# Writing out seven expert pairs of TensorE's program in place of a loop

## What is computed

```python
def expert_choice_ffn(h, w_router, w_gate, w_up, w_down):
    cap = EC_CAPACITY_FACTOR * T // N_EXPERTS          # 64 latent, 32 context tokens an expert
    aff = softmax(einsum('btd,de->bte', h, w_router))
    gate, idx = lax.top_k(swapaxes(aff, 1, 2), cap)
    xs = h[idx]
    hid = silu(xs @ w_gate) * (xs @ w_up)
    y = (hid @ w_down) * gate[..., None]
    return zeros.at[idx].add(y)
```

## Time and profile before

| What | Value |
|---|---|
| Median of 3 runs | 2056.06 us (2052.41 to 2056.16) |
| The profiled execution: time, span of its instructions | 2060.62 us, 2058.8 us |
| TensorE busy | 1944.4 us (94% of the span) |
| Mean granted TensorE clock | 0.975 |
| Layer 0's looped pairs, first matmul to first matmul of the eighth | 816.33 to 1117.11 us |
| Layer 0's eighth pair up to its `c` matmuls | 1117.11 to 1163.80 us |
| TensorE instruction queue (q8) | 109 packets, 1.79 MB |

### The profile page before, as it was taken

One profiled execution on the slowest core, in us unless ns is written; L12 is line 12 of the kernel. 1 busy time (PEld: TensorE's weight loads), 2 busy tenths in 40 slices (PEclk: granted clock), 3 DMA queues, 4 the chain that ended last, 5 costly groups with the idle time before them and its releaser, 6 DMA issues.

```text
span 2058.8 us, 41161 instructions
## 1 busy us (share of the span) xinstructions
PE 1944.4 (94%) x17601; PEld 1266.4 (62%) x17601; DVE 724.5 (35%) x1507; ACT 507.0 (25%) x1079; POOL 362.7 (18%) x411
## 2 busy tenths in 40 slices
PE   6999999899999998999999899999889999999998
PEld 4565567678888554555555445556688885455554
DVE  3154344344443334111121325334345442523223
ACT  4211533432222222010100131343332222210001
POOL 1512000333341002200010032100135330000000
PEclk7999999999999999999999999999899999999999
DMA  9410000344444215999999612100100002489996
GB/s 326 126 41 21 21 1 1 114 158 153 149 141 145 73 51 175 310 347 312 328 325 316 229 41 62 42 0 21 53 13 13 23 3 104 162 342 408 414 408 263
DMA packets 196888, 320.65 MB, mean 156 GB/s; under 512 B 10761, under 2 KB 163119, under 8 KB 189583
## 3 DMA queue, kind: packets, MB, share of 16 engines
q1 hardware_dynamic: 184928, 287.20, 39.6%
q0 software_dynamic: 6432, 20.00, 3.5%
q10 hardware_dynamic: 5390, 11.44, 1.6%
HBM read 305.45 MB, written 13.16 MB: 155 GB/s over the span
## 4 chain that ended last, share of the span: by engine, by line
PE 82%; DMA 5%; DVE 5%; ACT 4%; issue 2%; SPq 1%; POOL 1%; DVEq 0%; ACTq 0%; POOLq 0%
PE psum L564 16%; PE psum L962 7%; PE psum L1104 5%; PE psum L1056 5%; PE psum L1082 5%; PE psum L684 3%; PE psum L1167 3%; PE psum L893 3%; DMA ring<-in_moe_w_up 3%; PE psum L905 3%; PE psum L1063 2%; PE psum L908 2%; PE psum L729 2%; PE psum L704 2%; PE psum L501 2%
## 5 line engine op out<-in xcount | busy, mean ns | idle before, releaser
L564 PE MATMUL psum<-hT,ring 128*128 128x256 f32 (+2 forms) x976 | 336.8, 502 | 4.2 <-ACT hT L1481 3.8
L564 PEld LDWEIGHTS psum<-hT,ring 128*128 128x128 f32 (+1 forms) x976 | 184.0, 191 | 144.5 <-issue 126.8
L1056 PE MATMUL psum<-ring,arena 128*64 128x256 f32 x1024 | 126.4, 403 | 25.3 <-DMA ring<-in_moe_w_up 15.2
L962 PE MATMUL psum<-hT,ring 128*128 128x512 f32 (+1 forms) x384 | 139.4, 521 | 0.9 <-DVE xT L2261 0.9
L905 PE MATMUL psum<-ring,wbuf 64*64 64x64 f32 x1920 | 123.3, 226 | 3.7 <-DVE wbuf L2226 2.8
L908 PE MATMUL psum<-wbuf,ring 64*64 64x64 f32 x1920 | 121.1, 224 | 0.0
L2533 POOL TENSOR_TENSOR mlaw<-ring,lev 128x512 f32<-128x512 f32 x72 | 91.1, 1270 | 165.0 <-PE psum L893 162.6
L1056 PEld LDWEIGHTS psum<-ring,arena 128*64 128x64 f32 x1024 | 76.3, 145 | 68.8 <-issue 36.7
L2348 DVE TENSOR_TENSOR arena<-arena,psum 128x384 f32<-128x384 f32 (+1 forms) x32 | 15.6, 488 | 291.1 <-PE psum L1063 191.7
L962 PEld LDWEIGHTS psum<-hT,ring 128*128 128x128 f32 x384 | 72.7, 190 | 64.8 <-issue 61.5
L905 PEld LDWEIGHTS psum<-ring,wbuf 64*64 64x64 f32 x1920 | 103.8, 140 | 7.3 <-issue 5.3
(11 more groups left out here) (330 smaller groups left out, 3294.3 us busy)
## 6 DMA issues: line engine op xcount, KB each, us to landing
ring<-in_moe_w_gate SPq DMA_DIRECT2D x64, 1024.0 KB, 10.1
ring<-in_ada_w SPq DMA_DIRECT2D x48, 1024.0 KB, 5.2
ring<-in_moe_w_up SPq DMA_DIRECT2D x48, 1024.0 KB, 8.1
ring<-in_moe_w_down SPq DMA_DIRECT2D x32, 1024.0 KB, 11.2
ring<-in_w_in SPq DMA_DIRECT2D x20, 1024.0 KB, 5.9
big<-in_moe_w_down SPq DMA_DIRECT2D x16, 1024.0 KB, 14.5
ring<-in_w_out SPq DMA_DIRECT2D x8, 1024.0 KB, 5.1
xT<-in_moe_w_up SPq DMA_DIRECT2D x8, 1024.0 KB
```

The costliest lines, as they stand in the source:

```text
L564: m = pe.matmul(b[0:c1 - c0, 0:n], lhsT=w[:, k, c0:c1], rhs=hT[:, k, t0:t0 + n], start=k == 0, stop=k == KD - 1)
L962: m = pe.matmul(b[:, 0:x], lhsT=w[:, k, c:c + P], rhs=mixT[:, k, t0:t0 + x], start=k == OUT_REST[0], stop=k == OUT_GDN[-1])
L1056: m = pe.matmul(b[e * CAP_L:(e + 1) * CAP_L, 0:2 * P], lhsT=xs[:, k, e, 0:CAP_L], rhs=w[e][:, k, :], start=k == 0, stop=k == KD - 1)
```

## The change

The body of TensorE's loop becomes a function, `looped(i)`. In layer 0 (`need_ctx`) it is called seven times by Python with the numbers 0 to 6, so the instructions stand in the program seven times with constant thresholds. Layer 1 keeps the loop. No other engine's program differs except for line numbers.

```diff
-                with pe.Fori(0, PAIRS - 1) as i:
+                def looped(i):
+
                     def claim2(name):
...
                     pair(claim2, done2, weights2, free2, lambda name: ("moe", l, name), i,
                          i * per_pair + 2 * per_pair)
+
+                if need_ctx:
+                    for i in range(PAIRS - 1):
+                        looped(i)
+                else:
+                    with pe.Fori(0, PAIRS - 1) as i:
+                        looped(i)
                 for b in range(BANKS):
                     uses[b] += (PAIRS - 1) * per[b]
```

## The result

The written-out kernel takes 2057.86 us at the median of 20 runs (2049.91 to 2062.91), the kernel before 2052.53 us at the median of 20 beside it (2047.27 to 2058.60). The ratio is 1.0023 with a 95% interval of 1.0012 to 1.0033: 4.7 us slower, 2.5 to 6.8. The profiled execution of after took 2058.16 us, its span is 2056.3. It happens to be quicker than the profiled execution of before, the other way round than the medians. Single runs of one kernel scatter by some 4 us, so the difference is looked for inside the pairs, not between two spans.

The account below looks back on a forecast made before the run. The prediction took each pair to be paced by a closed ring through u0, u1's load and VectorE's additions. Terms 0 + 0.6 − 0.6 + 0.9 = +0.9 us on the 2056.06 us median gave 2057.0 us, range 2050 to 2068.

Parts of the forecast that it names:

- the clock: After some u1 waits the granted clock falls, 1.69 us each; up to three more or fewer, ±5.1 us.
- The branch: Six back edges and one exit removed in layer 0, covered by VectorE's additions: 0, at most 3.0 us.
- The form of g0's wait: Constant thresholds make six inner boundaries start g0 0.14 us after VectorE's addition instead of 0.04: +0.6 us.
- The form of u1's wait: Landing to u1's first matmul takes 0.14 us instead of 0.23, in seven pairs: −0.6 us.
- More code to fetch: 23 more 16 KB code packets add traffic on busy DMA engines: +0.9 us, bounds 0 and 8.4.
- Fetches delay u1's load: Rival: packets make u1's loads land late, up to 1.4 us a pair; with clock falls +13.5 us, 2069.6; chance 0.17.
- Nothing else is idle: In the seven pairs TensorE idles only before u1 (15.2 us) and before g0 at back edges (3.0 us).
- Back edges were dear after all: Rival: idle time at back edges and 0.23 us at u1 all go, −4.6 us, 2051.5; chance 0.13.
- A fetch at the back edge: Rival: each of six returns to the loop's head fetches a packet; writing out saves 7.2 us, 2048.9; chance 0.02.
- TensorE starves at the fetches: Rival: TensorE stops for each of 23 packets, 27.6 us slower, 2083.7; chance 0.04.
- the ring: What paces a layer 0 pair: u0 done, load issued, landed, u1, rest of pair, VectorE's additions, next g0, u0.

Follow-up runs that it names:

- e1_null: The kernel before, unchanged, timed again against itself: ratio 0.9999 (0.9982 to 1.0016), −0.7 us.
- e5_mimic_h0: The looped kernel before plus, in each of layer 0's seven looped pairs, a 16.3 KB copy on ScalarE's queue behind h0: 1.0003, +1.1 us.
- e6_mimic_g0: The looped kernel before plus, in each of layer 0's seven looped pairs, a 16.3 KB copy on ScalarE's queue behind g0: 1.0014, +2.4 us.
- e2_again: The written-out kernel, unchanged, timed again against the kernel before: ratio 1.0014 (0.9996 to 1.0031), +2.6 us.
- e3_both: The written-out kernel with TensorE's loop written out in layer 1 too; against the kernel before 1.0017 (1.0 to 1.0034), +4.2 us.
- e4_single_loops: The written-out kernel with each of layer 0's seven pairs a one-pass loop ending in a branch not taken; against the kernel before 1.0013, +2.4 us.
- e10_place_bad: The written-out kernel plus 9 small matmuls before u1 in seven pairs and 55 ahead of pair 1, setting where fetches fall: 1.0024, +3.8 us.
- e12_warm: The looped kernel before plus one 512-column matmul (four in pair 8) ahead of u1's wait in layer 0: 0.9982 (0.9965 to 0.9999), −3.4 us.
- e8_half_loop: The looped kernel before with only half the columns of each layer 0 down weight loaded: 1.0008 (0.9992 to 1.0025), +1.6 us.
- e7_two_pairs: TensorE's layer 0 as pair 1 written out, then three loop passes of two pairs, thresholds in registers; against the kernel before 1.0073, +15.0 us.

## Why the prediction was right, and which term was off

The forecast was 2057.0 us for a measured 2057.86, and slower by 0.9 us for a measured 4.7 (2.5 to 6.8). That the two times agree within 0.9 us is luck. The forecast started from 2056.06 us, the median of three runs, and the same kernel had 2052.53 in the 20 runs beside after: the start was 3.5 us too high, and the effect 3.8 us too small (4.4 by the medians). The measured ratio lies just beyond the 0.2% that the text took as the limit, and its interval leaves out no change; so by the text's own measure the outcome is "slower", to which it gave 0.22, and not "same" with 0.63. The range of 2050 to 2068 held because it was made wide for the clock and the rivals. Over the three comparisons of this change (20, 12 and 12 runs: +4.7, +2.6, and +2.4 with the branches) the mean, weighted by runs, is +3.5 us. The traces point the same way: pairs 2 to 7 without falls are 251.0, 248.6, 250.2 and 247.9 us in four looped kernels (before, e1_null, e5_mimic_h0, e6_mimic_g0), mean 249.4, and 252.6, 251.4, 253.0 and 252.5 in four written out (after, e2_again, e3_both, e4_single_loops), mean 252.4. That is 3.0 us where 0.9 was forecast.

**The branch, 0: right.** VectorE's additions cover it; the boundary waits for them before and after, and branches put back (e4_single_loops) win nothing.

**The form of g0's wait, +0.6: right.** 0.59 us in place of 0.50 at six boundaries, +0.54.

**The form of u1's wait, −0.6: right in sign, somewhat too small, and not seen in the sum.** By the records of landings the first matmul follows the last share by 0.23 us in every looped pair of before, e1_null, e5_mimic_h0 and e6_mimic_g0, and by 0.09 in every written-out one of after, e2_again, e3_both and e4_single_loops (in pair 2 of after 880.05 and 880.14). So each u1 starts 0.14 us sooner, 1.0 us in seven. The 0.14 us that the text took from the earlier trace rows stands at u1 only where a small matmul goes before it, as in the chain of e10_place_bad at pair 3:

```profile
916.32 7.99 DMA ring<-in_moe_w_up
924.31 0.14 issue
924.45 1.70 PE psum L1063 x13
```

The looped e12_warm has the same 0.14 us with its thresholds in registers, so with a matmul in front of the wait the form makes no difference. The six waits before u1 add up to 12.2, 9.8, 11.3 and 8.9 us in the four written-out kernels, against 11.9, 9.4, 12.0 and 9.3 in the four looped ones: means of 10.5 and 10.6. The 0.8 us that the form gives in six pairs have gone again. u1's second load takes 7.43 us from issue to landing in the mean where the looped kernels have 7.30, which is 0.8 us in six pairs, but single traces range from 7.1 to 7.7 either way.

**More code to fetch, +0.9: the term that was mis-sized, and in the wrong place.** The 23 packets came exactly, and TensorE doesn't starve at them; that the traffic among the loads costs something was right. The term was half of a mean share over 16 engines. What the traces show is one late share: a packet takes about 1 us of one engine, and a load has landed only with its last share. The text had this as a rival, "Fetches delay u1's load", and looked for it at u1, where it measures 0.13 us a pair and not the 0.7 from which it was to decide; the load that shows it is the next one. In the looped kernels the second down load lands only 0.2 to 0.6 us before L1104 is ready for it, and 2.0 to 2.3 us before it only where u1 has run at the lower clock. L1104 follows u1 without idle time in all 30 looped inner pairs traced in before, e1_null, e5_mimic_h0, e6_mimic_g0 and e12_warm, and waits above 0.2 us in one to three of six pairs in every written-out one with whole loads. In the four written-out kernels TensorE's idle time before L1104, waits of 0.1 us and less with it, is 1.3, 1.4, 1.8 and 2.7 us, mean 1.8. With the 0.54 of g0 that makes 2.4 of the 3.0 us. The remaining 0.6 isn't before u1, whose waits are equal. It lies in stretches that the views call busy: from u0 to g1 the written-out kernels take 0.8 us over the least time in six pairs and the looped ones 0.3, and up to L1104 another 0.2. Why is not known; "Nothing else is idle" in the prediction overlooked such stretches.

**The late share.** The sixteen landings of each load, read from the records, tell more than the waits. Take how far the last share lags behind the fifteenth, for the second down load, less the same lag of u1's second load, which lands just before: this is the lag that is new. In 36 looped pairs (before, e1_null, e5_mimic_h0, e6_mimic_g0, e8_half_loop, e12_warm) it is never above 0.2 us. In the six kernels written out with whole loads 29 of 36 pairs have a packet of code between 0.8 us before u1's start and 3.95 behind it. In 13 of these the new lag is 0.3 to 1.6 us, and those are the 13 pairs that wait 0.2 us or more before L1104 (up to 1.25); in the seven pairs without such a packet it is at most 0.1 us, and none waits. In each of the 13 the other fifteen shares had landed 0.5 to 1.4 us before L1104 was ready. The bounds of that stretch were chosen after the traces were seen.

**The rivals.** "Back edges were dear after all" and "A fetch at the back edge" fall with the boundaries of 0.59 us. The second needs a longer body (e7_two_pairs). "TensorE starves at the fetches" falls: no new idle time inside a run of matmuls. The clock isn't the cause: mean 0.976 over the 12 runs of e1_null and of e2_again, three falls in before, one in e1_null, two in after, none in e2_again. As the text said, it is the largest part of the scatter.

**What stays open.** That the waits before L1104 come with code fetched in that stretch is shown by their presence in all six kernels written out with whole loads, with or without branches, and in e7_two_pairs with its registers, and by their absence in all kernels whose loop is kept. That a single packet makes them, through one late share, rests on the records: each wait above 0.2 us, those of e7_two_pairs with it, has a packet between 0.7 us before u1's start and 3.9 us behind it. It was not brought about by itself: the copies didn't do it, and moving the packets changed little. Another cause in the written-out program (D) is left only so far as it comes and goes with the fetching, since e4_single_loops has the branches back and e7_two_pairs the registers. Sixteen of the 29 pairs with a packet there don't wait. Shares land 1 to 2 us late in looped kernels too, from another source; u1's load is then as late as the down load, and u1 starts later with it. Which engine the packet falls on may decide; the records here don't name the engine. And the 4.7 us of the timed runs are more than the 3.0 of the traces, which is within the scatter.

**A word on the ring ahead of the prediction.** Both loads for u1 go into slots that g0 frees (`slot_full5` and `slot_full4` stand at g0 and at u1). The second is issued only behind u0 because SP's program makes it wait for that (`m == 1` in the loop at L1400), not because its slot is taken. The closed ring through u0 is thus a choice of the program. No run changed it.

## What to carry to other kernels

Writing out a loop on an engine whose back edge already lies behind another engine's work saves nothing, and it puts the code itself among the transfers: where a load is waited for, ask which load lands just in time, not what the mean share of the DMA engines is. Keep a loop body small enough to be kept: one pair here, not two. Where an engine waits for a load at a known place, a spare matmul in that wait is worth a try for the clock: here it gave 0.18%, just clear of the noise. And when a forecast and a measurement agree, lay the differences beside each other and not the times, for the start may have moved as much as the effect.

## What the runs showed of the hardware

- A loop body of 1,003 recorded TensorE instructions is kept between passes (one packet in six pairs, 0.50 us at the back edge). One of 2,004 isn't: each back edge has 6.1 us of idle time, of which 3.9 lie between the branch (943.37 us in e7_two_pairs) and the first packet (947.30).
- Packets of code of 16 KB took 0.9 to 1.4 us, median 1.1 in after; the longest of any trace took 2.1 (e1_null). A copy's packets of 960 bytes took 44 ns.
- With the DMA engines at about 1.0 and a load waited for in each pair, code fetched next to it went with one share of sixteen landing 0.3 to 1.6 us later than before, in 13 of 29 pairs. With the engines as busy and no load waited for (layer 1), nine packets cost nothing (30.04 against 30.12 us a pair).
- With a 512-column matmul in a wait of 1 to 3 us no u1 of six pairs fell to the lower clock, where looped traces without it have none to three; the mean granted clock of the timed runs was 0.978 against 0.976. The six waits came to 6.0 us in place of 9.3 to 12.0, with the matmul in the time that is gone from them. The whole was 0.18% faster, by an interval that just leaves out no change (0.9965 to 0.9999).
- The form of a wait moves the start behind it by a tenth of a microsecond, either way: at g0's bank 0.14 us after VectorE's addition with a constant threshold and 0.04 with one in a register; at u1's weights 0.09 us after the landing with a constant and 0.23 with a register operation in between; 0.14 in both forms when a filler matmul stands in front of the wait.
